# Feed-forward projections of unnormed rows, and a recurrent stage scaled by a diagonal

## The reference

```python
def rms_norm(x, g):
    y = xf * lax.rsqrt(jnp.mean(xf * xf, -1, keepdims=True) + EPS)
    return (y * g.astype(jnp.float32)).astype(x.dtype)

def conv_ffn(x, w_up, conv_w, conv_b, w_down):
    u = x @ w_up                          # 1024 -> 2 x 2816
    up = jnp.pad(u, ((0, 0), (1, 1), (0, 0)))
    c = conv_b
    for j in range(3):                    # a convolution over neighbouring tokens
        c = c + conv_w[j] * up[:, j:j + s]
    g, val = c[..., :2816], c[..., 2816:]
    return (jax.nn.gelu(g) * val) @ w_down

h = h + rms_norm(mixer(rms_norm(h, g0)), g1)
h = h + rms_norm(conv_ffn(rms_norm(h, g2), ...), g3)
```

## Time and profile before

| | |
|---|---|
| median of 3 runs | 1056.98 us |
| profiled execution | 1056.94 us |
| its span | 1055.1 us, mean granted PE clock 0.999 |
| PE busy | 1026.9 us, 97% |
| DVE busy | 667.6 us, 63% |
| ACT busy | 557.1 us, 53% |
| POOL busy | 418.1 us, 40% |

### The profile page before, as it was taken

How to read it: one execution, slowest core, us unless ns; L and a number is a source line. 1 busy time by engine, 2 the same in 40 slices (tenths; PEclk the granted TensorE clock), 3 DMA queues, 4 the chain that set the end, 5 groups by cost and what they waited for, 6 DMA issues and landing times.

```text
span 1055.1 us, 21644 instructions
## 1 busy us (share of the span) xinstructions
PE 1026.9 (97%) x8138; PEld 941.0 (89%) x8138; DVE 667.6 (63%) x1094; ACT 557.1 (53%) x1014; POOL 418.1 (40%) x283
## 2 busy tenths in 40 slices
PE   9999999999999999999999999999999999999997
PEld 7788699999978888699999987899999999999996
DVE  4555867767767766777676766766676555554445
ACT  5655665555564654665555556644543455554442
POOL 1000243334333443433343363865653375533331
PEclk9999999999999999999999999999999999999999
DMA  9334456566434443365655624333213245446551
GB/s 354 102 120 140 159 182 206 188 201 191 151 138 160 156 135 128 124 210 184 201 191 167 205 77 160 104 119 120 81 62 121 81 140 157 151 135 215 195 181 42
DMA packets 46284, 161.82 MB, mean 153 GB/s; under 512 B 5264, under 2 KB 6544, under 8 KB 46096
## 3 DMA queue, kind: packets, MB, share of 16 engines
q1 hardware_dynamic: 45072, 156.79, 44.7%
q0 software_dynamic: 1152, 4.19, 1.2%
HBM read 159.91 MB, written 1.05 MB: 153 GB/s over the span
## 4 chain that ended last, share of the span: by engine, by line
PE 89%; DVE 5%; ACT 2%; POOL 2%; issue 1%; DMA 0%; DVEq 0%; SPq 0%; ACTq 0%
PE work L411 13%; PE work L413 13%; PE work L412 13%; PE work L1849 9%; PE acc L411 6%; PE acc L412 6%; PE acc L413 6%; PE work L2567 4%; PE work L2579 3%; PE acc L2579 2%; PE acc L2096 1%; PE acc L2110 1%; PE acc L2112 1%; PE acc L1941 1%; PE work L1387 1%
## 5 line engine op out<-in xcount | busy, mean ns | idle before, releaser
L380 POOL TENSOR_TENSOR low<-raw,high 128x1024 fp32r<-128x1024 f32 x110 | 269.0, 2449 | 276.5 <-ACT high L367 274.0
L380 DVE TENSOR_TENSOR low<-raw,high 128x1024 fp32r<-128x1024 f32 (+1 forms) x185 | 271.0, 1473 | 147.9 <-ACT high L367 147.8
L367 ACT ACTIVATE high<-raw 128x1024 fp32r<-128x1024 f32 (+2 forms) x295 | 298.6, 1026 | 36.6 <-DMA raw<-in_w_out 23.7
L411 PE MATMUL work<-xh,high 128*128 128x256 f32 (+1 forms) x1032 | 290.0, 281 | 2.1 <-DVE v_sb L1534 1.7
L412 PE MATMUL work<-xl,high 128*128 128x256 f32 (+1 forms) x1032 | 287.9, 279 | 0.0
L413 PE MATMUL work<-xh,low 128*128 128x256 f32 (+1 forms) x1032 | 287.8, 279 | 0.0
L411 PEld LDWEIGHTS work<-xh,high 128*128 128x128 f32 (+1 forms) x1032 | 193.2, 187 | 9.0 <-issue 5.6
L412 PEld LDWEIGHTS work<-xl,high 128*128 128x128 f32 (+1 forms) x1032 | 193.3, 187 | 1.7
L413 PEld LDWEIGHTS work<-xh,low 128*128 128x128 f32 (+1 forms) x1032 | 193.3, 187 | 0.2
L1290 POOL TENSOR_TENSOR h<-gelu,cv 128x256 f32<-128x256 f32 x44 | 49.7, 1130 | 194.3 <-ACT gelu L1214 87.6
L1849 PE MATMUL work<-xh,high 128*128 128x256 f32 x256 | 76.7, 300 | 0.0
(11 more groups left out here) (402 smaller groups left out, 2172.5 us busy)
## 6 DMA issues: line engine op xcount, KB each, us to landing
raw<-in_w_ffn SPq DMA_DIRECT2D x130, 512.0 KB, 4.3
raw<-in_w_out SPq DMA_DIRECT2D x39, 512.0 KB, 4.3
raw<-in_w_att SPq DMA_DIRECT2D x32, 512.0 KB, 3.9
raw<-in_w_diff SPq DMA_DIRECT2D x31, 512.0 KB, 3.9
raw<-in_w_gdn SPq DMA_DIRECT2D x24, 512.0 KB, 4.4
raw<-in_w_mla SPq DMA_DIRECT2D x8, 512.0 KB, 3.7
raw<-in_w_gdnz SPq DMA_DIRECT2D x8, 512.0 KB, 4.0
raw<-in_w_mla SPq DMA_DIRECT2D x8, 384.0 KB, 3.3
```

The costliest lines, as they stand in the source:

```text
L367: act.activation(high[k][:, 0:w], raw[k][:, 0:w], ACT.Copy).then_inc(high_done[k], 1)
L380: eng.tensor_tensor(low[k][:, 0:w], raw[k][:, 0:w], high[k][:, 0:w], ALU.subtract).then_inc(low_done[k], 1)
L411: pe.matmul(out, lhs[0], rhs[0], start=start, stop=False)
```

## The change

Boundaries 0 and 2 now go the raw way too, and the factor is made for all three. In a feed-forward each projected half is multiplied in place in PSUM by the row of roots on DVE (`scaled`) before ACT reads it for the middle tap. PE computes the factor between up(0) and up(1) of step 0. DVE's splits are put in other places of the step. Boundary 3 turns and scales rows in one product, `hid` by a diagonal matrix of roots, and the gates use a bank of `acc`. The gain rows and their DMAs are gone. Waits on `xl` are finer, semaphore counts of the taps go from 2 to 3 per step. The number of spins differs by boundary.

```diff
-            if arriving == RAW and b % 2 == 0:
-                pe.wait_ge(n_["xl"], 4 * RAW + 1 + b // 2)
-            elif arriving is not None and b % 4 == 0:
-                pe.wait_ge(n_["xl"], 4 * arriving + 2 + b // 2)
+            if arriving is not None and b % 2 == 0:
+                pe.wait_ge(n_["xl"], split_seen(arriving) + b + 2)
...
     def pre_pe(pe, n):
+
         pe.wait_ge(g["const"], 48)
-        spin(pe, W[3][:], 7)
-        for t in range(NT):
-            for half in range(2):
-                pe.wait_ge(n_["hn"], 4 * (n - 1) + 2 * t + half + 1)
-                for b in range(4):
-                    at = (4 * half + b) * P
-                    last = pe.transpose(work[:, 2 * t + half, b * P:(b + 1) * P], hn[:, t, at:at + P], ident)
+        spin(pe, W[3][:], 6)
+        for half in range(2):
+            for t in range(NT):
+                pe.wait_ge(n_["hn"], HN_SEEN[n] + t + 1)
+                for b in range(4 * half, 4 * half + 4):
+                    last = pe.matmul(raw_turned(b)[:, t * P:(t + 1) * P], hid[:, t, b * P:(b + 1) * P], diag[t],
+                                     start=True, stop=True)
                 last.then_inc(n_["turned"], 1)
-        spin(pe, acc[:, 3, :], 1)
...
-    def pre_norm(dve, n, t, half):
+    diag = [hn[:, t, 0:P] for t in range(NT)]
+
+    def pre_diag(dve, n, t):
         dve.wait_ge(n_["root"], 2 * n + t + 1)
-        if t == 0 and half == 0:
-            dve.wait_ge(n_["gain"], 16 * (n if n < RAW else n - 1))
-        c = cols(half)
-        dve.scalar_tensor_tensor(hn[:, t, c], hid[:, t, c], stat[:, 8 + t:9 + t], pre_gain[:, c], ALU.mult,
-                                 ALU.mult).then_inc(n_["hn"], 1)
-
-    RAW = 2
-
-    def raw_pe(pe):
+        dve.tensor_scalar(diag[t], ident, stat[:, 8 + t:9 + t], None, ALU.mult).then_inc(n_["hn"], 1)
+
+    RAW = (1, 2, 3)
+
+    RAW_SPINS = {1: (4, 2, 2), 2: (0, 2, 1), 3: (4, 2, 2)}
+
+    def raw_pe(pe, n):
+        ahead, between, behind = RAW_SPINS[n]
+        if ahead:
+            pe.wait_ge(g["const"], 48)
+            spin(pe, W[3][:], ahead)
         for t in range(NT):
             if t == 1:
-                spin(pe, acc[:, 0, :], 2)
+                spin(pe, acc[:, 0, :], between)
             for half in range(2):
-                pe.wait_ge(n_["hid"], 4 * (RAW - 1) + 2 * t + half + 1)
+                pe.wait_ge(n_["hid"], 4 * (n - 1) + 2 * t + half + 1)
                 for b in range(4):
                     at = (4 * half + b) * P
                     last = pe.transpose(raw_turned(4 * half + b)[:, t * P:(t + 1) * P], hid[:, t, at:at + P], ident)
                 last.then_inc(n_["turned"], 1)
-        spin(pe, acc[:, 3, :], 1)
+        spin(pe, acc[:, 3, :], behind)
...
+    def pre_split_act(act, n, half):
+        act.wait_ge(n_["turned"], 4 * n + (2 + half + 1 if n in RAW else 2 * half + 2))
         for b in range(4 * half, 4 * half + 4):
-            ins = act.activation(xh[:, b, :], raw_turned(b), ACT.Copy, scale=vcol("diff_gain", b, 1))
-            if b % 2:
-                ins.then_inc(n_["xh"], 1)
-
-    def raw_split_dve(dve):
+            act.activation(xh[:, b, :], raw_turned(b), ACT.Copy, scale=turned_gain(n, b)).then_inc(n_["xh"], 1)
+
+    def pre_split_dve(dve, n):
         for b in range(KB):
             if b % 2 == 0:
-                dve.wait_ge(n_["xh"], 4 * RAW + b // 2 + 1)
-            ins = dve.scalar_tensor_tensor(xl[:, b, :], raw_turned(b), vcol("diff_gain", b, 1), xh[:, b, :], ALU.mult,
-                                           ALU.subtract)
-            if b % 2:
-                ins.then_inc(n_["xl"], 1)
+                dve.wait_ge(n_["xh"], split_seen(n) + b + 2)
+            dve.scalar_tensor_tensor(xl[:, b, :], raw_turned(b), turned_gain(n, b), xh[:, b, :], ALU.mult,
+                                     ALU.subtract).then_inc(n_["xl"], 1)
...
+    def factor_mean_dve(dve, n):
+        pre_mean(dve, n, 1)
+        factor_cols_dve(dve, n)
...
-        if n in (0, RAW):
-            pool.wait_ge(n_["hn"], 4 * n + 4)
-            pool.dma_start(pre_gain[:], dram["pre_gain"][1 if n == 0 else 2]).then_inc(n_["gain"], 16)
...
-        step(0)
+        up(0, 0)
+        factor_pe(pe, 2 * layer + 1)
+        up(1, 0)
...
-                act.wait_ge(used[bank], p.base[bank] + i + 1)
+                act.wait_ge((s["g_tap"], s["v_tap"])[value], 3 * (i + done) + 1)
...
-        def block(j, i):
-            for value in range(2):
-                bank, s = 2 * j + value, f[j]
-                mid, tap, c = (s["g_mid"], s["v_mid"])[value], (s["g_tap"], s["v_tap"])[value], (cg, cv)[value][j]
-                dve.wait_ge(mid, i + done + 1)
-                dve.scalar_tensor_tensor(c[:, 1:TOK], W[bank][:, 0:TOK - 1], ffn_taps(layer, i, j, value, 0, 0),
-                                         c[:, 1:TOK], ALU.mult, ALU.add).then_inc(tap, 1)
-                dve.wait_ge(tap, 2 * (i + done) + 1)
-                dve.scalar_tensor_tensor(c[:, 0:TOK - 1], W[bank][:, 1:TOK], ffn_taps(layer, i, j, value, 2, 0),
-                                         c[:, 0:TOK - 1], ALU.mult, ALU.add).then_inc(tap, 1)
-                if not (is_last(i) and j == 1):
-                    refill(split, p, bank, i)
+        def scaled(j, value, i):
+            bank, tap = 2 * j + value, (f[j]["g_tap"], f[j]["v_tap"])[value]
+            dve.wait_ge(used[bank], p.base[bank] + i + 1)
+            dve.tensor_tensor(W[bank][:, 0:TOK], W[bank][:, 0:TOK], factor, ALU.mult).then_inc(tap, 1)
+
+        def tapped(j, value, i):
+            bank, s = 2 * j + value, f[j]
+            mid, tap, c = (s["g_mid"], s["v_mid"])[value], (s["g_tap"], s["v_tap"])[value], (cg, cv)[value][j]
+            dve.wait_ge(mid, i + done + 1)
+            dve.scalar_tensor_tensor(c[:, 1:TOK], W[bank][:, 0:TOK - 1], ffn_taps(layer, i, j, value, 0, 0),
+                                     c[:, 1:TOK], ALU.mult, ALU.add).then_inc(tap, 1)
+            dve.wait_ge(tap, 3 * (i + done) + 2)
+            dve.scalar_tensor_tensor(c[:, 0:TOK - 1], W[bank][:, 1:TOK], ffn_taps(layer, i, j, value, 2, 0),
+                                     c[:, 0:TOK - 1], ALU.mult, ALU.add).then_inc(tap, 1)
 
         def step(i):
-            block(0, i)
+            scaled(0, 0, i)
+            if not is0(i):
+                refill(split, p, 3, i - 1)
+            tapped(0, 0, i)
+            scaled(0, 1, i)
+            refill(split, p, 0, i)
+            tapped(0, 1, i)
             if is0(i):
                 if layer == 0:
                     split(p, 5, 0)
             elif not (is_last(i) and layer == 0):
                 refill(split, p, 4, i - 1)
-            block(1, i)
+            scaled(1, 0, i)
+            refill(split, p, 1, i)
+            tapped(1, 0, i)
+            scaled(1, 1, i)
+            if not is_last(i):
+                refill(split, p, 2, i)
+            tapped(1, 1, i)
             if not is0(i) and not (is_last(i) and layer == 0):
                 refill(split, p, 5, i - 1)
             if is_last(i):
                 for bank in (2, 3):
                     refill(split, p, bank, i)
 
+        factor_dve(dve, 2 * layer + 1)
...
-        boundary_dve(dve, 0, ph["mla"], 2)
+        boundary_raw_dve(dve, 0, ph["mla"], 2)
         refill(lo_of(dve), ph["mla"], 2, HEADS - 1)
+        factor_mean_dve(dve, 1)
         split_low(dve, False, ph["ffn0"], 4, 0)
         ffn_dve(dve, 0)
```

More of the change, by code:

```diff
@@ L492, in build @@
     g = sems("g", "x second_x const")
-    n_ = sems("n", "hid sq mean root hn turned xh xl gain")
+    n_ = sems("n", "hid sq mean root hn turned xh xl")
     h = sems("h", "qkev s mx sm e p pt ptev vev pv oh ol rope roped turned turned_ev")
@@ L550, in pre_square @@
                            accum_out=stat[:, 16 + 2 * t + half:17 + 2 * t + half]).then_inc(n_["sq"], 1)
[L552 to L555, removed]
     def pre_mean(dve, n, t):
@@ L616, in factor_pe, with factor_dve @@
         last.then_inc(n_["hn"], 1)
-    def factor_dve(dve):
-        dve.wait_ge(n_["hn"], 4 * (RAW - 1) + 3)
+    def factor_dve(dve, n):
+        dve.wait_ge(n_["hn"], HN_SEEN[n] + 3)
         dve.tensor_copy(factor, acc[:, 3, 0:TOK]).then_inc(n_["hn"], 1)
-        dve.wait_ge(n_["hn"], 4 * (RAW - 1) + 4)
-    def pre_split_dve(dve, n):
-        for half in range(2):
-            for t in range(NT):
-                dve.wait_ge(n_["xh"], 4 * n + 2 * t + half + 1)
-                dve.tensor_tensor(x_part(xl, t, half), turned(t, half), x_part(xh, t, half),
-                                  ALU.subtract).then_inc(n_["xl"], 1)
+        dve.wait_ge(n_["hn"], HN_SEEN[n] + 4)
     def pre_pool(pool, n, t):
@@ L708, in pre_act_split @@
     def pre_act_split(act, n):
-        for t in range(NT):
-            pre_split_act(act, n, t)
+        for half in range(2):
+            pre_split_act(act, n, half)
     def pre_dve(dve, n):
-        pre_norm(dve, n, 0, 0)
+        pre_diag(dve, n, 0)
         pre_mean(dve, n, 1)
```

(33 more changed lines are left out.)

59 lines of the change are left out of this document (33 added, 26 removed).

## The result

The changed kernel took 1114.13 us (median of 4 runs, 1113.92 to 1114.37), the kernel before 1057.14 in the same session (1056.97 to 1057.75): the ratio is 1.0536, 95% interval 1.0523 to 1.0549. It is slower by 57 us. I had forecast 1100.5 with a range of 1083 to 1112: the direction and the mechanism hold, the time lies 2 us outside the range, and 13.6 us were not in the sum. The profiled execution has a span of 1112.2.

The account below looks back on a forecast made before the run. PE bounds the kernel, the ring DVE, POOL, ACT coming second and overtaking it after the change. 24.4 + 21.0 - 0.9 - 0.9 + 0 = 43.6 on 1056.94 gives 1100.5 us, range 1083 to 1112 (its own 1093 to 1107).

Parts of the forecast that it names:

- The ring: Feed-forward steps: closed wait chain DVE, POOL, ACT, DVE, walked twice per step, recurring after 16.42 us, 0.27 below PE's step.
- The ring's length, 18.7 us: Feed-forward step after the change: low5 recurs every 18.7 us against PE's 16.69, so PE waits 2.0 per step.
- 0.07: First half of the feed-forward step: each of two hand-overs around ACT's middle tap, behind scaling g, takes 0.07 us.
- The bound of 19.0: Feed-forward ring: its length in us if each scaling takes 0.48 until DVE's next issue; with 0.28 it is 18.5.
- -4 and +5: Both feed-forward layers: the scaling's bounds move the 1100.5 us forecast by these us, to 1093 to 1107.
- rule on the drain: DVE issues only once the previous pipe is empty: each scaling costs 0.42, ring 19.0, time about 1106 us.
- Low1 costs 1.13 and POOL gives back 0.9: Feed-forward step: low1, moved out of the ring's wait, adds 1.13 us; POOL, no longer held behind it, wins 0.9.
- When it begins: First feed-forward: ring 7.0 us late at step 2, PE waits 0.5 there, then 2.0 in each of steps 3 to 9.
- The stall in step 1: First feed-forward: PE waits 3.3 us for low1's bank, delayed behind low5 and a scaling.
- The boundaries: Both boundaries into the feed-forwards: first product 1.7 us earlier, net 0.9 won each; into the recurrent stage 0, bounds -0.6 and +0.8.
- Rival three, the clock: PE's clock falls in the feed-forward stalls, PE's step 25 instead of 18.7, 100 us more, 1200 in all; chance 3%.
- the sum: Whole kernel: feed-forwards 24.4 and 21.0, boundaries -0.9 each, recurrent boundary 0, together 43.6 us more.

Follow-up runs that it names:

- experiment 3: The changed kernel without its 4 scalings per step, middle taps waiting for TensorE again: 1067.41 us, ratio 1.0093.
- experiment 5: The changed kernel with the ring opened: ACT's hh and high part, DVE's low5 and low4 later, POOL's low3 earlier, all scalings kept: 1069.34 us, ratio 1.0111.
- experiment 8: The changed kernel with two scalings moved into the ring's waits, one ahead of low4, one ahead of low5: 1082.35 us, ratio 1.0236.
- experiment 2: The changed kernel with 160 bytes left empty behind the table of vectors, tiles back at their old places modulo 256 bytes: 1109.13 us, ratio 1.0483.
- experiment 4: The changed kernel with low1 back behind the taps of the first half, in the shadow of the ring's wait: 1127.88 us, ratio 1.0661.

## Why the prediction was right or wrong

**The ring is the second bound: right.** It was read from two idle times with a releaser other than PE, and experiments 3, 5 and 8 show it from three sides.

**The ring's length, 18.7 us: 0.3 short, the first step that failed, and the larger one.** The mechanism was right and a term was mis-sized: the two hand-overs (from one engine's end to the next one's start) between scaling, middle tap and taps. Laid side by side, all places of the forecast agree within 0.02 us but one, which shifts all behind it: from the scaling's issue to the tap's I had 1.11 and it is 1.40 (239.65 to 241.05), since the two hand-overs take 0.25 and 0.16 and not 0.07 each. In the second feed-forward the ring is 19.10. Over 8 or 9 steps this is 2.4 us in the first stage and 3.4 in the second. The bound of 19.0 that I worked out was for slower scalings; I gave the hand-overs none, and the 0.07 stood there without a row. (Nor does the prediction's own range, 1093 to 1107, follow from its -4 and +5: taken once they give 1096.5 to 1105.5, taken for each layer 1092.5 to 1110.5.) The Trainium skill's rule on the drain ("VectorE: DVE Perf Modes", "The DRAIN you can't avoid"), cited in the prediction, would also have given 19.0, but not for the reason seen: the low part behind the second scaling is issued at 242.41, before the scaling's end (242.49).

**Low1 costs 1.13 and POOL gives back 0.9: right**, by experiments 3 and 4.

**When it begins: half right.** Steps are counted from 0, as in the prediction. The stall in step 1 is there (2.55, forecast 3.3). The later ones came in earnest from step 5 on (0.09 in step 4) and not from step 3. The slower products, which delay PE by themselves, account for one of these steps: with the tiles placed (2) the first later wait is 1.07, in step 4. The rest is that the ring was less late than forecast: in step 2, low5 comes 4.87 us behind the start of the first projection (160.40 and 155.53; 5.14 in experiment 2) and not 7.0. The fall of the clock behind the first stall, at 141.2, delays PE alone and would make 1.7 of that; this is argued. The stage's length does not hang on it: counted from the stage's first product, that low5 stands at 38.4 us, and by the forecast's terms at 39.0 (27.97 to step 2 before, 3.3, 0.45, 0.3 and 7.0). Some of PE's waits for the ring from there on, first feed-forward:

```profile
211.69 0.39 PE L409 MATMUL work<-xh,high 128*128 128x256 f32 x1 [1.81 <-DVE low L378]
...
230.70 0.39 PE L409 MATMUL work<-xh,high 128*128 128x256 f32 x1 [0.25 <-DVE low L378]
...
249.72 0.38 PE L409 MATMUL work<-xh,high 128*128 128x256 f32 x1 [1.78 <-DVE low L378]
```

These three are 19.0 us apart whatever the wait is; the place, ahead of the second projection, is the one forecast.

**The boundaries: right** (-1.80 and -1.77 against -1.7; boundary 3 costs 0.3 with the tiles placed, within the bounds given).

**Rival three, the clock: real, but small.** The granted clock fell from its 2.4 to its 1.2 GHz level 8 times before the very end of the span (at 141.2, 212.9, 250.5, 315.3, 561.1, 619.1, 656.6 and 680.5), for some 3.4 us each; PE had ended a wait of 1.8 to 2.6 us shortly before, or was still in it (680.5). Before the change it fell only at the very end. I had priced it at 100 us. The waits above show why it costs almost nothing inside a stage: at 212.9 the clock falls, PE loses 1.7 us (half of 3.4), and its next wait is 0.25 instead of 1.8. The ring sets the pace, and PE pays out of its idle time. At the end of the second feed-forward nothing is behind to absorb it. Windows around 250 and around the closing products of the second feed-forward, then these products:

```profile
250.00:254.00 4.00, 4.00 (x23) 4.00 (x23) 2.88 (x6) 2.05 (x4) 0.70 (x1) 0.57 0.77 290
...
680.60:684.10 3.50, 3.49 (x9) 2.78 (x10) 2.38 (x3) 2.52 (x5) 2.75 (x2) 0.52 0.00 0
```

```profile
681.60 1.05 PE L454 MATMUL acc<-low,hh 128*128 128x512 f32 x2
...
684.07 0.63 PE L454 MATMUL acc<-low,hh 128*128 128x512 f32 x2
```

Here it costs up to 1.7 us, once; what the fall at 315.3, near the end of the first, cost was not separated. The Trainium skill, "TensorE: Matmul & The Clock Gate", section "HAM oscillation", describes a cold start behind each wait; the trace agrees in part, since of PE's 14 waits of over 1 us in the two stages 8 were followed by a fall, and the price depended on whether anything else bounded the loop.

**The second step that failed: "the sum", in what it left out.** It held no term for the table of vectors growing by 24 columns. I had read that line of the change as data and costed it at nothing. It costs 11.7 us alone in the kernel before and 5.0 in the changed one, where the ring hides the rest. Of the 13.6 us missing, 5.0 are this, 5.8 the hand-overs (an estimate, 0.3 and 0.38 a step), up to 1.7 the clock at the second stage's end; about 1 us, most of it at the end of the second feed-forward (the wait for low4 and what follows it), I did not resolve. Without the placement the time would have been 1109.1, inside the range and 8.6 above the forecast.

## What to carry to other kernels

An engine's idle time is room only if no ring closes over it: ask of every wait who releases the releaser, and if the answer is the engine itself, new work belongs into the wait and not beside it (against experiment 3, which leaves them out, the 4 scalings cost 47 us in one order, 15 in a second, 2 in a third). In such a ring count each hand-over between engines at what the trace shows for that pair, not at the smallest one seen. And where a kernel has empty pads between its tiles, treat any change of a tile's size as a possible change of PE's pace: compare the pitch of untouched products in an untouched stage before explaining anything else.

## What the runs showed of the hardware that was not expected

- The pitch of 256-column products of two fp32r operands depends on where the moving rows (xh, xl) start: 116.7 ns at 32 bytes over a multiple of 256 from the weight tiles, 119.9 at 0 and 118.7 to 120.0 at 128; that of 512-column products lay between 226.8 and 234.6 ns, by which tiles had moved. Moving nothing but addresses changed the time by 0.3% to 1.1%.
- A fall of the clock's level for 3.4 us was free in a stage whose pace another engine set: steps of 19.0 us followed each other with waits of 1.8 or 0.25.
- A 128-column operation of DVE (0.29 us) took 2.98 when POOL's low part ran beside it, and with the clock's drop behind it 4.4 us were lost at one boundary.
